# RWKV-7 inverse on one core: VectorE transposes 32-row blocks in place of half of TensorE's products

## The chip, the cores and the metric

One Trainium2 chip; the kernel is one program on one NeuronCore. The metric is the device time of one execution in microseconds. The times given are of single executions, with their median.

## The reference, cut to what matters

The program computes two transformer-like blocks on 272 tokens (256 and 16 learned ones), width 1024, in float32. The part that the change touches is the recurrence of the RWKV-7 time mix of the first block, with 16 heads of 64:

```python
def step(S, inp):
    r_t, w_t, k_t, v_t, a_t, b_t = inp
    sa = jnp.einsum("bhij,bhj->bhi", S, a_t)
    S = S * w_t[:, :, None, :] + sa[..., None] * b_t[:, :, None, :] + v_t[..., None] * k_t[:, :, None, :]
    y = jnp.einsum("bhij,bhj->bhi", S, r_t)
    return S, y
```

The kernel doesn't step through tokens. It takes them in chunks of 16, 128 and 128 and solves, for each head and chunk, one triangular system: with L the strictly lower triangular matrix of the products of a and b inside a chunk, it needs X = (I - L)^-1, applied to the part of `sa` that earlier chunks and the keys give.

## The kernel before

**Groups and chunks.** The 16 heads go in four groups g of four (q = 0 to 3). Each group has three chunks: c = 0 with 16 tokens, c = 1 and 2 with 128. `rk_score` makes the products, `rk_mask` (VectorE) masks them into `rk_lb` and `rk_lk`, and `rk_levels` builds the inverse by doubling the block: level n joins blocks of 2^n rows into blocks of 2^(n+1). For chunks of 128 both 64-row halves (TOP and BOTTOM) are inverted side by side in levels 0 to 5, and level 6 joins them. Chunk 0 has levels 0 to 3.

**What a level does.** Both the inverse so far and its transpose are kept: `rk_x` and `rk_xt`, tiles of 128 x (4 heads x 64) for chunks 1 and 2. Lines here are those of kernel.py.
- Level 0: VectorE writes `rk_xt` from the masked products (`rk_begin`, L2266, two products, a drain, an addition of the identity). TensorE transposes it by a product with the identity (`rk_under` at n = 0, L808), and ScalarE copies the result from PSUM to `rk_x` (L1706).
- Levels 1 to 4: TensorE makes `rk_lb` times `rk_x` (`rk_under`, L806); VectorE masks it from PSUM into `rk_ym` (L2292); TensorE makes two products of it (`rk_merge`), o (L826), what is added to `rk_x`, and ot (L828), what is added to `rk_xt`; VectorE adds both (L2308 and L2309). `rk_under` of the next level waits for `rk_x` alone, `rk_merge` of the next level for `rk_xt` too.
- Level 5 is alike, with o for the TOP half only, and the transpose goes to `rk_upper` and `rk_lower`. Level 6 is one product each way, with copies at L2290 and L2300.

Every float32 product stands in the trace as two LDWEIGHTS and two MATMUL instructions. Additions and masks on VectorE go through a helper and carry line L2001 (L2004 for three operands), copies and activations on ScalarE L1420.

**What sets the order.** Each engine runs its instructions in the order in which its own program issues them. `beside(host, guest)` weaves two generators: the host is `rk_levels(g)`, which yields once after each chunk's under and merge (slots), and the guest `rk_beside(g)` gives a slot number before each piece. TensorE and VectorE have a host and a guest each. For group g the guests carry the chain of group g-1 through its three chunks (`rk_right` L867, `rk_solve` L880 to L883, `rk_update` L896 to L898, `rk_output` L917 to L921, and for statistics `rk_mean` L930 and `rk_variance` L937), and they prepare group g+1 (`rk_turn` L764, `rk_score` L781, on VectorE `rk_mask` and `rk_begin`). In group 0 VectorE's guests are six pieces of `rk_prepare`, one of them due at each of slots 1 to 6. From group 2 on there is `rk_finish` of group g-2, with two reciprocals (L2341). `rk_output` waits for VectorE's `rk_state`, `rk_score(.., 1)` for VectorE's mask of `rk_score(.., 0)`. `fill` (L746) issues products that nothing reads: in group 0 four of them before each chunk of level 0, and some later.

**Around it.** The weights come by DMA through a ring of four slots; while the inverse runs no weight is consumed, and the ring is full. After group 3 the linear layers go on, each engine in its own order.

Of the kernel before, what the change touches and what calls it, by code (L numbers as in the profile page):

```python
# [12 lines left out]
ALU = mybir.AluOpType  # L13
# [203 lines left out]
def build(nc, stream, x_in, params, consts, decay, out):  # L217
    with ExitStack() as ctx:
# [209 lines left out]
        def rk_level_bank(c, i):  # L428


            C, B = CHUNKS[c][1], RK_SIDE[c]
            bank, at = ((4, 64 * i), (max(i - 1, 0), 0), (2 + max(i - 1, 0), 0))[c]
            return ps[0:C, bank, at:at + 4 * B].rearrange("p (q t) -> p q t", q=4)
# [24 lines left out]
        def masked(g, c, i):  # L458
            return MASKS.index((g, c, i)) + 1
# [105 lines left out]
        def _(pe):  # L565
# [219 lines left out]
            def rk_under(g, c, n):  # L785

                C = CHUNKS[c][1]
                if n == 0:
                    pe.wait_ge(S[f"rk_xt{c}_begun"], g + 1)
                    if g == 0:  # L790
                        pe.wait_ge(S["rk_masked"], masked(g, c, 1))
                    if c == 0 and g >= 2:
                        pe.wait_ge(S["rk_y_rooted"], g - 1)
                elif n == 1:
                    pe.wait_ge(S[f"rk_x{c}_begun"], g + 1)
                else:
                    pe.wait_ge(S[f"rk_x{c}_added"], g * RK_COUNT[c] + 2 * n - 2 - (c > 0))
                settle(C)
                o, lb, x = rk_level_bank(c, 0), rk_lb[g % 2][c], rk_x[c]
                for q in range(4):  # L800
                    if n == LEVELS - 1:
                        mm = pe.matmul(o[BOTTOM, q, :], lb[TOP, q, 0, BOTTOM], x[TOP, q, :], start=True, stop=True)
                    else:
                        for b in RK_BLOCKS[c]:
                            if n:
                                mm = pe.matmul(o[b, q, :], lb[b, q, 0, b], x[b, q, :], start=True, stop=True)  # L806
                            else:
                                mm = pe.matmul(o[b, q, :], rk_xt[g % 2][c][b, q, :], ident[b, b], start=True, stop=True)  # L808
                mm.then_inc(S[f"rk_under{c}_ready"], 1)

            def rk_merge(g, c, n):

                C, nl = CHUNKS[c][1], RK_LEVELS[c]
                if n > 1:
                    pe.wait_ge(S[f"rk_x{c}_added"], g * RK_COUNT[c] + 2 * n - 2)
                pe.wait_ge(S[f"rk_under{c}_masked"], g * (nl - 1) + n)
                settle(C)
                o, ot, xt, y = rk_level_bank(c, 1), rk_level_bank(c, 2), rk_xt[g % 2][c], rk_ym[c]
                for q in range(4):
                    if n == LEVELS - 1:  # L820
                        mm = pe.matmul(ot[TOP, q, :], y[BOTTOM, q, :], rk_lower[g % 2][c][BOTTOM, q, :],
                                       start=True, stop=True)
                        continue
                    for b in RK_BLOCKS[c] if n < nl - 1 else ():
                        if n < LEVELS - 2 or b == TOP:
                            pe.matmul(o[b, q, :], xt[b, q, :], y[b, q, :], start=True, stop=True)  # L826
                    for b in RK_BLOCKS[c]:
                        mm = pe.matmul(ot[b, q, :], y[b, q, :], xt[b, q, :], start=True, stop=True)  # L828
                mm.then_inc(S[f"rk_merge{c}_ready"], 1)

            def rk_levels(g):

                for n in range(LEVELS):
                    chunks = [c for c in RK_ORDER if n < RK_LEVELS[c]]
                    for c in chunks:
                        if g == n == 0:
                            fill(4, 4)
                        if n == LEVELS - 1:
                            pe.wait_ge(S["rk_masked"], masked(g + 1, 2, 1) if g < 3 else len(MASKS))
                            fill(7, 4)  # L840
                        rk_under(g, c, n)
                        yield
                    for c in chunks if n else ():
                        rk_merge(g, c, n)
                        yield
# [572 lines left out]
        def _(act):  # L1418
            def copy(o, i, scale=1.0):
                return act.activation(o, i, ACT.Copy, scale=scale)  # L1420
# [280 lines left out]
            for c in range(3):  # L1701
                rk_turned(0, c)
            for g in range(4):
                for c in RK_ORDER:
                    act.wait_ge(S[f"rk_under{c}_ready"], g * RK_LEVELS[c] + 1)
                    copy(rk_x[c][0:CHUNKS[c][1], :, :], rk_level_bank(c, 0)).then_inc(S[f"rk_x{c}_begun"], 1)  # L1706
                for c in range(3):
                    if c and g < 3:
                        rk_turned(g + 1, c - 1)
                    if g:  # L1710
                        rk_solved(g - 1, c)
                        rk_out(g - 1, c)
                if g < 3:
                    rk_turned(g + 1, 2)
                else:
                    copy(rk_lora[:, :, :], rk_gate_first)
                if g:
                    rk_spread(g - 1)
# [280 lines left out]
        def _(dve):  # L1999
            def tt(o, a, b, op):  # L2000
                return dve.tensor_tensor(o, a, b, op)  # L2001
# [264 lines left out]
            def rk_begin(g, c):  # L2266


                C, B, xt = CHUNKS[c][1], RK_SIDE[c], rk_xt[g % 2][c]
                dve.drain()  # L2270
                for b in RK_BLOCKS[c]:
                    tt(xt[b, :, :], rk_lb[g % 2][c][b, :, 0, b], tokens_of(const("level_0t")[b, 0:B], 4), ALU.mult)
                if c and g < 2:
                    dve.memset(rk_upper[g][c][BOTTOM, :, :], 0.0)
                dve.drain()
                tt(xt[0:C, :, :], xt[0:C, :, :], tokens_of(const("eye")[0:C, 0:B], 4), ALU.add
                   ).then_inc(S[f"rk_xt{c}_begun"], 1)

            def rk_levels(g):

                xt, upper, lower = rk_xt[g % 2], rk_upper[g % 2], rk_lower[g % 2]
                for c in RK_ORDER:
                    yield
                for n in range(1, LEVELS):
                    chunks = [c for c in RK_ORDER if n < RK_LEVELS[c]]
                    for c in chunks:
                        C, B = CHUNKS[c][1], RK_SIDE[c]
                        dve.wait_ge(S[f"rk_under{c}_ready"], g * RK_LEVELS[c] + (n + 1))
                        if n == LEVELS - 1:
                            ins = dve.tensor_copy(rk_ym[c][BOTTOM, :, :], rk_level_bank(c, 0)[BOTTOM, :, :])  # L2290
                        else:
                            ins = tt(rk_ym[c][0:C, :, :], rk_level_bank(c, 0), tokens_of(level[0:C, n, 0:B], 4), ALU.mult)  # L2292
                        ins.then_inc(S[f"rk_under{c}_masked"], 1)
                        yield
                    for c in chunks:
                        C = CHUNKS[c][1]
                        dve.wait_ge(S[f"rk_merge{c}_ready"], g * (RK_LEVELS[c] - 1) + n)
                        o, ot = rk_level_bank(c, 1), rk_level_bank(c, 2)
                        if n == LEVELS - 1:
                            ins = dve.tensor_copy(lower[c][TOP, :, :], ot[TOP, :, :])  # L2300
                        elif n == LEVELS - 2:
                            tt(rk_x[c][TOP, :, :], o[TOP, :, :], rk_x[c][TOP, :, :], ALU.add
                               ).then_inc(S[f"rk_x{c}_added"], 1)
                            tt(upper[c][TOP, :, :], ot[TOP, :, :], xt[c][TOP, :, :], ALU.add)
                            ins = tt(lower[c][BOTTOM, :, :], ot[BOTTOM, :, :], xt[c][BOTTOM, :, :], ALU.add)
                        else:
                            if n < RK_LEVELS[c] - 1:
                                tt(rk_x[c][0:C, :, :], o, rk_x[c][0:C, :, :], ALU.add).then_inc(S[f"rk_x{c}_added"], 1)  # L2308
                            ins = tt(xt[c][0:C, :, :], ot, xt[c][0:C, :, :], ALU.add)  # L2309
                        ins.then_inc(S[f"rk_x{c}_added"], 1)  # L2310
                        yield

# [100 lines left out]
            for c in range(3):  # L2413
                rk_mask(0, c, 1)
                if c:
                    rk_begin(0, c)
            rk_begin(0, 0)
            for g in range(4):
                beside(rk_levels(g), rk_beside(g))
# [396 lines left out]
```

## Time and profile before

| | us |
|---|---|
| times of three executions | 2116.26, 2116.26, 2118.11 |
| median | 2116.26 |
| the profiled execution, its own time | 2117.51 |
| its span in the trace | 2115.7 |
| granted TensorE clock, mean share of full speed | 0.979 |
| the inverse, from the first L808 to the last L821, on the span's clock | 353 to 530 |

The profile has an engine's busy time, the chain that ended last, groups of instructions, and a timeline. In a timeline row the number in brackets is how long the engine sat idle before the row and what it then waited for; a row merges neighbours of the same line, "x16" counting them. The end of a TensorE instruction is modelled, so the distance between starts is what it costs in a stream. "In group 2" means from 441.0 to 488.6 us.

### The profile page before, as it was taken

How to read it: one execution, taken by the hardware profiler on the slowest of the kernel's cores; microseconds unless marked ns; L12 is line 12 of the kernel's file. 1: busy time of each engine (PE TensorE's matmuls, PEld its weight loads, DVE VectorE, ACT ScalarE, POOL GpSimd, SP SyncE). 2: the span in 40 equal slices, each digit the busy share in tenths (PEclk: the TensorE clock that was granted, in tenths of full speed). 3: DMA queues.
4: the chain of work that ended last, by engine and by line, in shares of the span. 5: the costliest groups of instructions: out<-in, count | busy, mean ns of one | idle time of the engine just before them, and what ended most of it. 6: DMA issues, size and time to landing. Idle time of an engine off the chain costs nothing.

```text
span 2115.7 us, 43855 instructions
## 1 busy us (share of the span) xinstructions
PE 2011.4 (95%) x17474; PEld 1893.6 (90%) x17474; DVE 1056.3 (50%) x1608; ACT 924.2 (44%) x1613; POOL 1278.4 (60%) x528
## 2 busy tenths in 40 slices
PE   7999998999999999999989999999999989999997
PEld 7999687788899999998966999999998868898997
DVE  5770677566678617842474686030453243325431
ACT  4334552111343444344436444344446545656552
POOL 6887361000388877885720788776755544677885
PEclk9999999999999999999979999999999988999999
DMA  7444331000244544543310454543453332344552
GB/s 279 166 174 178 119 120 61 2 3 3 100 160 178 179 160 159 178 179 140 142 58 9 163 188 179 199 160 142 158 219 132 113 116 96 124 179 147 191 183 76
DMA packets 40935, 291.44 MB, mean 138 GB/s; under 512 B 4448, under 2 KB 5728, under 8 KB 5856
## 3 DMA queue, kind: packets, MB, share of 16 engines
q1 hardware_dynamic: 40656, 288.40, 37.7%
q8 instruction: 108, 1.77, 0.3%
q10 hardware_dynamic: 144, 1.05, 0.1%
q14 instruction: 27, 0.22, 0.0%
HBM read 288.38 MB, written 1.05 MB: 137 GB/s over the span
## 4 chain that ended last, share of the span: by engine, by line
PE 32%; issue 28%; POOLq 19%; POOL 18%; ACT 1%; DVE 1%; DMA 0%; DVEq 0%; SPq 0%; ACTq 0%
POOLq L1979 18%; POOL w_low L1975 18%; PE ps L617 10%; PE ps L625 9%; PE ps L621 9%; PE ps L1355 2%; PE ps L1343 1%; PE ps L1333 1%; PE ps L729 0%; POOLq L1974 0%; DMA X<-x_in 0%; ACT units L1881 0%; ACT units L1420 0%; POOLq L1991 0%; DVE units L2001 0%
## 5 line engine op out<-in xcount | busy, mean ns | idle before, releaser
L1975 POOL TENSOR_TENSOR w_low<-wring,w_high 128x1024 fp32r<-128x1024 f32 x524 | 1278.2, 2454 | 816.1 <-ACT w_high L1420 786.1
L617 PE MATMUL ps<-in_high,w_high 128*128 128x256 f32 (+1 forms) x2856 | 831.2, 291 | 33.8 <-DVE in_low L2001 12.9
L625 PE MATMUL ps<-in_high,w_low 128*128 128x256 f32 (+1 forms) x2856 | 820.7, 287 | 0.0
L621 PE MATMUL ps<-in_low,w_high 128*128 128x256 f32 (+1 forms) x2856 | 819.1, 287 | 0.0
L1420 ACT ACTIVATE w_high<-wring 128x1024 fp32r<-128x1024 f32 x524 | 542.2, 1055 | 278.1 <-PE ps L617 273.2
L617 PEld LDWEIGHTS ps<-in_high,w_high 128*128 128x128 f32 x2856 | 546.1, 191 | 46.6 <-issue 36.7
L625 PEld LDWEIGHTS ps<-in_high,w_low 128*128 128x128 f32 x2856 | 546.2, 191 | 0.0
L621 PEld LDWEIGHTS ps<-in_low,w_high 128*128 128x128 f32 x2856 | 545.8, 191 | 0.5
L617 PE MATMUL ps<-hid_high,w_high 128*128 128x272 f32 (+1 forms) x880 | 254.6, 289 | 0.0
L625 PE MATMUL ps<-hid_high,w_low 128*128 128x272 f32 (+1 forms) x880 | 250.4, 284 | 0.0
L621 PE MATMUL ps<-hid_low,w_high 128*128 128x272 f32 (+1 forms) x880 | 250.2, 284 | 0.0
L2001 DVE TENSOR_TENSOR hid_low<-hidden,hid_high 128x272 f32 (+1 forms) x88 | 215.7, 2451 | 13.0 <-issue 2.4
L2004 DVE SCALAR_TENSOR_TENSOR X<-ps,X 128x272 f32<-128x272 f32 (+1 forms) x64 | 27.7, 433 | 333.1 <-PE ps L625 333.1
L1561 ACT ACTIVATE silu_out<-ps 128x272 f32<-128x272 f32 (+1 forms) x88 | 34.7, 394 | 301.9 <-DVE ps L2001 301.9
L621 PEld LDWEIGHTS ps<-hid_low,w_high 128*128 128x128 f32 x880 | 165.7, 188 | 0.7
L617 PEld LDWEIGHTS ps<-hid_high,w_high 128*128 128x128 f32 x880 | 165.4, 188 | 0.7
L625 PEld LDWEIGHTS ps<-hid_high,w_low 128*128 128x128 f32 x880 | 165.5, 188 | 0.0
L2039 DVE CAST hid_high<-hidden 128x272 f32 (+1 forms) x88 | 97.0, 1103 | 17.2 <-issue 17.2
L2001 DVE TENSOR_TENSOR ps<-ps,rms 128x272 f32<-128x272 f32 (+1 forms) x176 | 73.9, 436 | 61.2 <-PE ps L625 60.0
L1420 ACT ACTIVATE AL<-ps 128x272 f32<-128x272 f32 (+5 forms) x95 | 39.7, 434 | 138.8 <-PE ps L625 46.6
L2004 DVE SCALAR_TENSOR_TENSOR conv_out<-ps,par,conv_out 128x255 f32<-128x255 f32 x88 | 42.5, 482 | 46.5 <-ACT conv_out L1550 37.7
L1508 ACT ACTIVATE units<-ps 128x256 f32<-128x256 f32 x69 | 26.4, 383 | 85.1 <-PE ps L625 85.0
(339 smaller groups left out, 2566.9 us busy)
## 6 DMA issues: line engine op xcount, KB each, us to landing
wring<-stream SPq DMA_DIRECT2D x270, 1024.0 KB, 4.8
con<-consts SPq DMA_DIRECT2D x1, 2199.0 KB, 16.0
X<-x_in SPq DMA_DIRECT2D x1, 1088.0 KB, 7.6
units<-decay ACTq DMA_DIRECT2D x1, 1024.0 KB, 4.8
out<-AL SPq DMA_DIRECT2D x1, 1024.0 KB, 4.7
AL<-stream SPq DMA_DIRECT2D x2, 256.0 KB, 19.7
par<-params SPq DMA_DIRECT2D x1, 187.0 KB, 4.9
con<-consts SPq DMA_DIRECT2D x1, 130.0 KB, 7.5
```

The lines of the kernel that those rows point to most:

```text
L617: mm = pe.matmul(o, wh, high(k), start=(k == 0), stop=False)
L621: mm = pe.matmul(o, wh, low(k), start=False, stop=False)
L625: mm = pe.matmul(o, wl, high(k), start=False, stop=(k == kt - 1))
L1355: mm = pe.matmul(ps[:, 7, :], v, pt.rearrange("p q t -> p (q t)"), start=(i == 0), stop=(i == len(of_keys) - 1))
L1420: return act.activation(o, i, ACT.Copy, scale=scale)
L1508: act.activation(put(i), ps[:, BANK[tile], 0:size], func(i)).then_inc(S["act_emptied"], 1)
L1561: act.activation(silu_out[:, p % 2, tokens], ps[:, (base + 2 * p) % 4, 0:size], ACT.Silu).then_inc(S["act_emptied"], 1)
L1975: pool.tensor_tensor(w_low[:, (half + h) % SPLIT_RING, :], wring[:, slot, h * HALF * P:(h + 1) * HALF * P], w_high[:, (half + h) % SPLIT_R ...
L1979: pool.drain()
L2001: return dve.tensor_tensor(o, a, b, op)
L2004: return dve.scalar_tensor_tensor(out=o, in0=a, scalar=scalar, in1=b, op0=op0, op1=op1)
L2039: dve.tensor_copy(hid_high[:, tile, tokens], hidden[:, p:p + 1, tokens])
```

## The change

Where the blocks have up to 32 rows, `rk_xt` of chunks 1 and 2 is got from `rk_x` (or at level 0 `rk_x` from `rk_xt`) by a transpose on VectorE, which turns each 32 x 32 block where it stands. At level 0 the 16 products with the identity and both ScalarE copies go, and `rk_first` (VectorE) writes `rk_x`: for group 0 before `rk_begin(0, 0)`, for later groups at level 6 of the group before, behind the copies of L2290. At levels 1 to 4 the products ot of chunks 1 and 2 go, and VectorE's addition to `rk_xt` is replaced by a drain and a transpose. Level 5, level 6 and chunk 0 keep what they do; chunk 0's block is written as rows 0 to 16 throughout. Semaphore counts follow.

```diff
@@ rk_under, TensorE
+                if n == (c > 0) and g == 0:
+                    pe.wait_ge(S["rk_masked"], masked(g, c, 1))
                 if n == 0:
-                    pe.wait_ge(S[f"rk_xt{c}_begun"], g + 1)
-                    if g == 0:
-                        pe.wait_ge(S["rk_masked"], masked(g, c, 1))
-                    if c == 0 and g >= 2:
+                    pe.wait_ge(S["rk_xt0_begun"], g + 1)
+                    if g >= 2:
                         pe.wait_ge(S["rk_y_rooted"], g - 1)
@@ rk_merge, TensorE
-                    for b in RK_BLOCKS[c] if n < nl - 1 else ():
-                        if n < LEVELS - 2 or b == TOP:
-                            pe.matmul(o[b, q, :], xt[b, q, :], y[b, q, :], start=True, stop=True)
+                    if n == LEVELS - 2:
+                        pe.matmul(o[TOP, q, :], xt[TOP, q, :], y[TOP, q, :], start=True, stop=True)
+                    elif c == 0 and n < nl - 1:
+                        pe.matmul(o[:, q, :], xt[0:C, q, :], y[0:C, q, :], start=True, stop=True)
                     for b in RK_BLOCKS[c]:
-                        mm = pe.matmul(ot[b, q, :], y[b, q, :], xt[b, q, :], start=True, stop=True)
+                        if c and n < LEVELS - 2:
+                            mm = pe.matmul(o[b, q, :], xt[b, q, :], y[b, q, :], start=True, stop=True)
+                        else:
+                            mm = pe.matmul(ot[b, q, :], y[b, q, :], xt[b, q, :], start=True, stop=True)
@@ rk_levels, TensorE
-                        rk_under(g, c, n)
+                        if n or c == 0:
+                            rk_under(g, c, n)
@@ the groups, ScalarE
-                for c in RK_ORDER:
-                    act.wait_ge(S[f"rk_under{c}_ready"], g * RK_LEVELS[c] + 1)
-                    copy(rk_x[c][0:CHUNKS[c][1], :, :], rk_level_bank(c, 0)).then_inc(S[f"rk_x{c}_begun"], 1)
+                act.wait_ge(S["rk_under0_ready"], g * RK_LEVELS[0] + 1)
+                copy(rk_x[0][0:CHUNKS[0][1], :, :], rk_level_bank(0, 0)).then_inc(S["rk_x0_begun"], 1)
@@ new, VectorE
+            def rk_first(g, c):
+                dve.transpose(rk_x[c], rk_xt[g % 2][c]).then_inc(S[f"rk_x{c}_begun"], 1)
@@ rk_levels, VectorE: behind the masks of a level
+                    if n == LEVELS - 1 and g < 3:
+                        dve.drain()
+                        for c in chunks:
+                            rk_first(g + 1, c)
@@ rk_levels, VectorE: behind the merge, levels 1 to 4
-                            ins = tt(xt[c][0:C, :, :], ot, xt[c][0:C, :, :], ALU.add)
+                            if c:
+                                dve.drain()
+                                ins = dve.transpose(xt[c], rk_x[c])
+                            else:
+                                ins = tt(xt[c][0:C, :, :], ot, xt[c][0:C, :, :], ALU.add)
@@ before group 0, VectorE
+            dve.drain()
+            for c in (1, 2):
+                rk_first(0, c)
             rk_begin(0, 0)
```

## Rows read from the trace of the kernel before

**Rows 1.** Busy time by engine, page of the profile, whole span.

```profile
PE 2011.4 (95%) x17474; PEld 1893.6 (90%) x17474; DVE 1056.3 (50%) x1608; ACT 924.2 (44%) x1613; POOL 1278.4 (60%) x528
```

**Rows 2.** Stretches: length, busy us (instructions) per engine, clock, DMA share, GB/s.

```profile
352.00:394.00 42.00, 34.73 (x702) 29.84 (x703) 32.57 (x78) 3.57 (x9) 0.00 (x0) 1.00 0.01 2
394.00:441.00 47.00, 44.94 (x864) 37.92 (x863) 25.90 (x65) 7.80 (x18) 0.00 (x0) 1.00 0.01 2
441.00:488.60 47.60, 45.54 (x874) 38.52 (x873) 30.86 (x71) 7.23 (x18) 0.00 (x0) 1.00 0.01 3
488.60:530.00 41.40, 38.94 (x813) 33.71 (x812) 24.74 (x61) 5.04 (x13) 0.00 (x0) 1.00 0.01 3
```

**Rows 3.** Groups by form, 352 to 530: count, busy us, mean ns, idle before.

```profile
L828 PE MATMUL ps<-group,in_parts 64*64 64x64 f32 x320 | 19.7, 220 | 0.0
```

**Rows 4.** Line 808: count, ns min/median/max, first and last start, forms.

```profile
L808 PE MATMUL ps<-con,group x80: 171/218/267, 352.8 to 443.3; 64*64 64x64 f32 x64, 16*16 16x16 f32 x16
```

**Rows 5.** TensorE timeline, group 2: start, us, what, idle before and releaser.

```profile
445.86 0.33 PE L826 MATMUL ps<-in_parts,group 64*64 64x64 f32 x4
...
446.94 0.29 PE L917 MATMUL ps<-in_parts 16*64 16x16 f32 x4
...
457.21 0.44 PE L917 MATMUL ps<-AL,in_parts 128*64 128x128 f32 x4 [0.48 <-DVE small L2001]
...
468.35 1.13 PE L781 MATMUL ps<-AL 64*128 64x256 f32 x8 [1.06 <-DVE AL L2001]
...
478.63 1.13 PE L781 MATMUL ps<-AL 64*128 64x256 f32 x8 [0.43 <-DVE AL L2001]
```

**Rows 6.** VectorE timeline, group 2, same columns.

```profile
447.05 0.76 DVE L2001 TENSOR_TENSOR group<-ps,group 128x256 f32<-128x256 f32 x2 [0.55 <-PE ps L828]
...
456.14 0.41 DVE L2001 TENSOR_TENSOR small<-ps,small 128x256 f32<-128x256 f32 x1
456.63 0.42 DVE L2001 TENSOR_TENSOR small<-small 128x256 f32<-128x256 f32 x1
...
467.08 1.22 DVE L2001 TENSOR_TENSOR AL<-ps,con 128x1024 f32<-128x1024 f32 x1
```

**Rows 7.** VectorE, bounds of one instruction: a short one and the longest.

```profile
351.98 0.27 DVE L2274 MEMSET group<- 64x256 f32 x1
...
L2341 DVE RECIPROCAL in_parts<-in_parts 128x272 f32<-128x272 f32 x5 | 9.2, 1849 | 0.1
```

**Rows 8.** VectorE, then TensorE, timelines at the start of group 0.

```profile
356.30 1.36 DVE L2001 TENSOR_TENSOR AL<-AL 128x544 f32<-128x544 f32 x2
...
367.61 0.76 DVE L2001 TENSOR_TENSOR group<-ps,group 128x256 f32<-128x256 f32 x2 [0.68 <-PE ps L828]
...
350.84 1.16 PE L746 MATMUL ps<-con 128*128 128x128 f32 x8
...
356.28 1.16 PE L746 MATMUL ps<-con 128*128 128x128 f32 x8
357.36 0.36 PE L808 MATMUL ps<-con,group 16*16 16x16 f32 x8
...
360.12 0.33 PE L826 MATMUL ps<-in_parts,group 64*64 64x64 f32 x4 [1.02 <-DVE in_parts L2001]
```

**Rows 9.** VectorE timeline where groups meet: 0 with 1, 2 with 3.

```profile
392.67 0.98 DVE L2290 COPY in_parts<-ps 64x256 f32<-64x256 f32 x2
393.92 0.97 DVE L2300 COPY group<-ps 64x256 f32<-64x256 f32 x2 [0.27 <-PE ps L821]
...
488.63 0.42 DVE L2300 COPY group<-ps 64x256 f32<-64x256 f32 x1 [1.29 <-PE ps L821]
```

**Rows 10.** Stretches before the inverse and where the clock fell, as rows 2.

```profile
346.00:350.00 4.00, 1.57 (x18) 1.00 (x20) 2.73 (x4) 0.00 (x0) 0.00 (x0) 1.00 0.00 0
...
993.00:995.00 2.00, 0.34 (x2) 0.00 (x0) 0.60 (x1) 1.35 (x2) 0.00 (x0) 1.00 0.30 127
995.00:997.00 2.00, 0.00 (x0) 0.00 (x0) 1.92 (x3) 0.13 (x1) 0.00 (x0) 0.72 0.00 0
```

More of the change, by code:

```diff
@@ L2275, in rk_begin @@
                 dve.drain()
-                tt(xt[0:C, :, :], xt[0:C, :, :], tokens_of(const("eye")[0:C, 0:B], 4), ALU.add
-                   ).then_inc(S[f"rk_xt{c}_begun"], 1)
+                ins = tt(xt[0:C, :, :], xt[0:C, :, :], tokens_of(const("eye")[0:C, 0:B], 4), ALU.add)
+                if c == 0:
+                    ins.then_inc(S["rk_xt0_begun"], 1)
+            def rk_first(g, c):
+                dve.transpose(rk_x[c], rk_xt[g % 2][c]).then_inc(S[f"rk_x{c}_begun"], 1)
             def rk_levels(g):
@@ L2287, in rk_levels @@
                         C, B = CHUNKS[c][1], RK_SIDE[c]
-                        dve.wait_ge(S[f"rk_under{c}_ready"], g * RK_LEVELS[c] + (n + 1))
+                        dve.wait_ge(S[f"rk_under{c}_ready"], g * RK_LEVELS[0] + n + 1 if c == 0 else g * (LEVELS - 1) + n)
                         if n == LEVELS - 1:
```

## The prediction

> **What bounds the kernel now.** The page first: TensorE is busy for 95% of the span, VectorE for half [rows 1]. That is an average over many stages, so I cut the inverse into its four groups [rows 2]. There is next to no DMA there, the granted clock is 1.00 throughout, and TensorE is busy 44.94 of 47.00 us in group 1, 45.54 of 47.60 in group 2 and 38.94 of 41.40 in group 3. VectorE has 24.7 to 30.9 us of work in these. Group 0 is another case: TensorE 34.73 of 42.00, VectorE 32.57. So three groups are bound by TensorE's stream of small products, and the first partly by VectorE. As TensorE's instructions run in program order, a product taken out lets everything behind it move up, until something behind it waits for VectorE. Those waits decide how much comes back; I read them in the timelines [rows 5, 6].
>
> **What goes.** The groups by form show 320 instructions of 64*64 at L828 for one buffer, and a second row with 320 for the other, the products ot of levels 1 to 5 [rows 3]: two chunks, four groups, 16 each per level, for five levels. Four of five levels go: 512. L808 has 64 of 64*64 in the even groups [rows 4] and as many in the odd ones: 128 more. In a stream such an instruction costs not its 220 ns but its distance to the next: merge of chunk 1 at level 1, 32 instructions (both products), begins at 445.86 and the next piece at 446.94 [rows 5]; less about 0.15 for its start and end, that is 0.93 us, 29 ns each. So 640 x 29 ns = 18.8 us of TensorE's stream go, 4.7 per group, 0.94 at each of levels 0 to 4. ScalarE's eight copies at level 0 go too; they are off the path, TensorE having other work meanwhile, and I give them nothing.
>
> **What comes.** VectorE gets 40 transposes of 128x256: 32 in place of additions, 8 new, each pair behind a drain. No row of before has a transpose. The bounds are a memset of 0.27 us and a reciprocal of 1.85 us [rows 7]. I take 0.42 us, the time of a plain 128x256 operation in the row at 456.63 [rows 6], since data go through once in both; both ends stay for the range. The Trainium skill (VectorE: DVE Perf Modes, "The three transpose paths") gives 311 ns for 128x128 in bf16; no run here shows that, and for twice the elements it would be an estimate between 0.31 and 0.62.
>
> A drain: two independent additions take 0.76 us together, so the second begins 0.34 behind the first; the pair with a drain between (456.14 and 456.63) is 0.49 apart [rows 6]. A drain costs 0.15, and the pair of an addition and a transpose 0.91 where the two additions took 0.76. The Trainium skill says otherwise (VectorE: DVE Perf Modes, "The DRAIN you can't avoid"): the pipe is emptied behind every operation anyway and chaining doesn't avoid it. By that rule the drains would be free, and the 32 of levels 1 to 4 would take 4.8 us less of VectorE than I reckon; with half of them on the path the gain would be 2.4 us larger. The rows contradict it here, and I go by them.
>
> **How much comes back: group 2, step by step.** I shift each piece by what is gone ahead of it and hold it where its releaser is late. *Level 0*: 0.94 gone, but `rk_solve` now stands close behind `rk_right` and waits for VectorE's copy between them; 0.6 come back. *Level 1*: another 0.94, but `rk_output` of chunk 0 waits 0.4 for the state, which stands behind VectorE's masks. The under of level 2 comes 1.5 earlier. *Level 2*: `rk_output` of chunk 1 (457.21) already waits 0.48 for `rk_state`, which stands behind chunk 1's additions [rows 5, 6]. These begin when chunk 1's merge ends, now 0.47 sooner, and take 0.15 more: it starts 1.8 earlier in all, TensorE waiting 1.4. *Level 3*: `rk_score` at 468.35 waits 1.06 for the mask that VectorE begins at 467.08, again behind chunk 1's additions [rows 5, 6]. It starts 2.15 earlier and waits 1.85. *Level 4*: VectorE had idled between chunk 1's and chunk 2's additions, so both halves of the merges count; `rk_score` at 478.63 starts 3.0 earlier. So 3.0 of 4.7 come back: 0.6 at level 0 and 2.4 behind it. The rule is that what is behind chunk 2's merge waits for VectorE work started by chunk 1's.
>
> *Group 1* has the same waits: 2.4 behind its level 0. *Group 3* has no preparation of a next group to fill TensorE, so after about 0.6 per level its chain under, mask, merge, addition becomes the bound: 0.6 + 2.2. *Ends of groups*: between L2290 and L2300 VectorE idles 1.29 us at the end of group 2, so drain and two transposes (0.9) are hidden. At the end of group 0 the idle is 0.27 [rows 9], and they cost 0.6.
>
> *Group 0* begins with a loss. VectorE's chain is the bound: `rk_prepare` at 356.30 runs on to the mask for which TensorE's merge at 360.12 waited 1.02 us [rows 8]. A drain, two transposes and `rk_begin` behind them put it 0.95 later. VectorE's next idle is before 367.61 [rows 8]; from there levels 2 to 4 bring 2.3, and the end takes 0.6 of 0.94 at level 0 of group 1. Net: -0.95 + 2.3 - 0.4 = +0.95.
>
> **Sum**: 0.95 + 2.4 + 3.0 + 2.8 = 9.15 us. Nothing behind the inverse hides it, as the weights lie ready and each engine goes on in order. The profiled execution took 2117.51 (span 2115.7), which gives 2108.4; it stands 1.25 above the median of 2116.26, so the median becomes **2107.1**.
>
> **Rivals.**
> *A. All comes back* (18.8 us, 2097.5). For it: TensorE's 95%. Against: TensorE already waits in three places per group for VectorE, and I only shorten the cover. Chance 0.07.
> *B. The transpose costs twice and more, and the gain is lost.* About five of ten transposes per group are on the path, 20 in all. At 0.72 us the gain falls by 6 to 3.1, at 0.88 it is nil. So from 0.66 to 1.1 us the time is within 4.2 us of before: 2112 to 2120. For it: nothing here shows the operation. Chance 0.14.
> *C. Slower through VectorE.* Place: the additions of levels 1 to 4; price: that of the reciprocal, 1.85 us. Then 20 x 1.43 = 28.6 more, less 9.15: 19.5 slower, 2135.7. It decides from 0.88 on and shows as slower from 1.1. Chance 0.06.
> *D. Slower through the clock.* The three `fill`s at level 0 (1.08 us each, 356.28 to 357.36) now run one after another from 350.84 [rows 8] to 354.1, since no product stands between them, and TensorE then idles until about 357.2, when `rk_begin(0, 0)` ends: 3.1 us, and again for some 2 us before the first merge, which moves from 360.12 to 361.1. In the trace the clock fell from 1.00 to 0.72 and on to its lower level (1.2 GHz) after TensorE had been busy 0.34 of 2 us and 0.00 of the next 2; it did not fall where it was busy 1.57 of 4 us [rows 10]. The Trainium skill (TensorE: Matmul & The Clock Gate, "Part 1: The HAM clock gate") has the same rule, that an idle TensorE is put back to half rate. So a fall is about as likely as not. Its price: at 1.2 GHz a stream of 29 ns products takes 58 ns, but until 367 VectorE is the bound and hides that, so I give it 0 to 2 us. It decides if the clock stays low for over 9 us of busy TensorE past 367; through all of group 0 it would cost up to 25 us, 16 more than is gained: 2132. Against: the products are dense there. Chance 0.06.
>
> **Numbers.** The forecast (gain 4.3 to 14) has 0.67, A 0.07, B 0.14, C 0.06, D 0.06. About 0.2% (4.2 us) is what a measurement of this kernel can tell from no change. Faster by more than that: 0.67 + 0.07 = 0.74; within: 0.14; slower: 0.12. The range leaves out the full return, C and D: from 2100 (16 back) to 2115.5, where the transpose costs 0.84.
>
> **What would show it.** L828 of 64*64 down from 640 to 128, none at L808. TRANSPOSE rows of about 0.42 us, 40 of them: 0.8 would mean B, over 1.1 C. The stretch from 353 to 530 shorter by 9, its group 2 by 3.0; TensorE's waits for VectorE up from about 2 to about 4 us in groups 1 and 2, at `rk_output` of chunk 1 1.4 and at `rk_score` 1.85. Group 0's first mask about 0.95 later, and the granted clock around 354 to 361 either 1.00 or at 1.2 GHz with no loss behind 367. Wrong would be: a stretch unchanged though transposes are short, or one shorter by 15 and more, or the difference outside this stretch.

## The result: slower, by the clock

The changed kernel took 2130.12 us in the median of four executions (2127.39 to 2133.25), before 2116.38; the ratio is 1.0063, with a 95% interval of 1.0046 to 1.0081. Ten more executions of it later gave 2127.29 (2119.05 to 2139.0) beside 2116.74, ratio 1.0059 (1.0035 to 1.0082). A ratio is the time of the kernel at hand over that of before on the same chip; all those below are within one per cent of 1, and what counts is whether their interval leaves 1 out. I had forecast 2107.1, faster.

The page of the changed kernel, parts 1 and 2, shows what moved:

```profile
PE 2012.9 (95%) x16834; PEld 1891.3 (89%) x16834; DVE 1060.3 (50%) x1616; ACT 921.8 (43%) x1605; POOL 1280.2 (60%) x528
...
PEclk9999998899899999999989999999999988999999
```

The 640 TensorE instructions are gone (17474 in [rows 1], 16834 here), and its busy time still grew, from 2011.4 to 2012.9 us. That is what a lower clock would do, and the stretches below show where it was low. The clock line has 8s in the seventh, eighth and eleventh slices, where the inverse runs and ends; in the profile of before the whole inverse had 1.00 [rows 2]. Stretches of the changed kernel, cut where the granted clock changes (length, busy us and count of PE, PEld, DVE, ACT, POOL, then clock, DMA share, GB/s):

```profile
346.90:350.30 3.40, 1.68 (x20) 0.86 (x16) 1.79 (x2) 0.00 (x0) 0.00 (x0) 1.00 0.00 0
...
350.30:357.10 6.80, 6.09 (x27) 5.27 (x28) 6.36 (x13) 0.00 (x0) 0.00 (x0) 0.50 0.00 0
...
394.70:398.10 3.40, 2.76 (x44) 2.49 (x44) 2.86 (x8) 0.21 (x1) 0.00 (x0) 1.00 0.00 0
398.10:411.80 13.70, 13.70 (x178) 11.92 (x176) 4.23 (x12) 1.42 (x4) 0.00 (x0) 0.50 0.01 2
...
425.40:428.80 3.40, 1.71 (x22) 1.30 (x24) 2.58 (x6) 0.00 (x0) 0.00 (x0) 1.00 0.00 0
428.80:432.20 3.40, 3.40 (x38) 2.42 (x34) 1.10 (x1) 0.38 (x1) 0.00 (x0) 0.50 0.00 0
447.40:492.20 44.80, 40.80 (x707) 33.80 (x706) 32.26 (x74) 6.29 (x15) 0.00 (x0) 1.00 0.01 2
...
493.70:497.10 3.40, 3.00 (x78) 2.65 (x77) 2.88 (x5) 0.59 (x2) 0.00 (x0) 1.00 0.02 5
497.10:507.30 10.20, 10.20 (x142) 9.38 (x144) 5.60 (x13) 0.58 (x2) 0.00 (x0) 0.50 0.01 2
534.60:548.30 13.70, 13.70 (x83) 10.31 (x84) 5.61 (x7) 2.33 (x5) 2.35 (x1) 0.50 0.00 0
```

At 0.50 the clock is at its lower level, 1.2 GHz. There TensorE is busy without a gap (13.70 of 13.70 us): it is the bound, at half speed. The falls come at starts of groups 1 and 3, in the middle of group 1, twice in group 0 and behind group 3. The first, at 350.30, lies ahead of every instruction that the change touches. The kernel before ran the same products there, 1.23 us earlier on its span's clock and as busy as the first row above, and kept its clock:

```profile
345.67:349.07 3.40, 1.68 (x20) 0.86 (x16) 1.80 (x2) 0.00 (x0) 0.00 (x0) 1.00 0.00 0
```

So one and the same stretch can be followed by a fall in one execution and not in another, and chance has a part here. The repeat of the changed kernel (e8 below) says so too: its profile has falls at the starts of groups 1 and 2 and none in group 3. What TensorE did before a fall is in the rows ahead of the 0.50 ones. It was half idle before two of them (1.68 and 1.71 busy us of 3.40). Before the falls at the starts of groups 1 and 3 it wasn't: 2.76 and 3.00 of 3.40, in small products with short waits.

Group 2 is the piece that had 1.00 throughout, and it did what was forecast. From one level 6 to the next (line L821), first before, then changed:

```profile
440.61 0.97 PE L821 MATMUL ps<-in_parts 64*64 64x64 f32 x13
...
487.92 0.97 PE L821 MATMUL ps<-group,in_parts 64*64 64x64 f32 x13
...
526.41 1.14 PE L821 MATMUL ps<-in_parts 64*64 64x64 f32 x16
```

```profile
447.41 1.14 PE L821 MATMUL ps<-in_parts 64*64 64x64 f32 x16
...
492.20 1.14 PE L821 MATMUL ps<-group,in_parts 64*64 64x64 f32 x16
```

47.31 us became 44.79, 2.5 less. In a second profile of the changed kernel (the repeat, e8) group 3 had the full clock, and 38.49 became 36.08, 2.4 less:

```profile
499.46 1.14 PE L821 MATMUL ps<-group,in_parts 64*64 64x64 f32 x16
...
535.54 1.14 PE L821 MATMUL ps<-in_parts 64*64 64x64 f32 x16
```

The waits are the forecast ones too: TensorE's idle time in group 2 is 4.00 us (44.80 less 40.80, the stretch from 447.40) where it was 2.06 [rows 2]. TensorE's timeline in group 2 of the changed kernel, to be held against [rows 5]:

```profile
462.52 0.44 PE L923 MATMUL ps<-AL,in_parts 128*64 128x128 f32 x4 [1.06 <-DVE small L2006]
...
473.38 1.13 PE L781 MATMUL ps<-AL 64*128 64x256 f32 x8 [1.71 <-DVE AL L2006]
...
482.91 1.14 PE L781 MATMUL ps<-AL 64*128 64x256 f32 x8 [0.62 <-DVE AL L2006]
```

**Time against the clock.** Every execution has its mean granted clock, and 2 x (1 - clock) x span is the time at the lower level, called low time from here on. The 97 executions of before that ran beside all these kernels have 72 to 110 us of it, mean 88, and their times, 2111.0 to 2123.8, rise by 0.45 us per us of it (a straight line fitted). The 14 of the changed kernel have 119 to 171 us, mean 142, slope 0.41. On these lines, at 85 us for both, before takes 2116.0 and the changed kernel 2104.8: 11.2 less. That is an extrapolation for the changed kernel, whose least is 119; by the scatter of its 14 points it is good to about 3 us. So two sizes stand against each other: 54 us more at the low level, at 0.45 each some 24 us, against 11 to 13 us less of work. The means of all executions are 2117.4 and 2128.2, 10.8 apart.

### The profile page after: what moved, and what is told of

Its sections match the earlier page's. It is cut to its first block, busy times and chain, and to the rows that moved or that the text cites. A ratio compares the mean times of both kernels' runs of the same rounds, so it can differ in the third digit from the quotient of the medians.

```text
span 2125.6 us, 42611 instructions
## 1 busy us (share of the span) xinstructions
PE 2012.9 (95%) x16834; PEld 1891.3 (89%) x16834; DVE 1060.3 (50%) x1616; ACT 921.8 (43%) x1605; POOL 1280.2 (60%) x528
## 4 chain that ended last, share of the span: by engine, by line
PE 31%; issue 28%; POOLq 19%; POOL 18%; ACT 1%; DVE 1%; DMA 0%; DVEq 0%; SPq 0%; ACTq 0%
POOLq L1984 18%; POOL w_low L1980 18%; PE ps L617 9%; PE ps L625 9%; PE ps L621 9%; PE ps L1361 1%; PE ps L1349 1%; PE ps L1339 1%; PE ps L729 0%; POOLq L1979 0%; DMA X<-x_in 0%; ACT units L1886 0%; ACT units L1426 0%; POOLq L1996 0%; DVE units L2006 0%
## 6 DMA issues: line engine op xcount, KB each, us to landing
AL<-stream SPq DMA_DIRECT2D x2, 256.0 KB, 18.6
```

## The experiments

Theory 1: the work is less, as forecast, and the loss is the granted clock. Theory 2, the rival: VectorE's drains, transposes and later start cost it, whatever the clock. Each kernel has one profile, of one of its executions, and it isn't always a typical one; where that matters it is said.

**e1, TensorE's products kept.** VectorE as changed; TensorE issues what the change had taken out, and nobody reads it.

```diff
                         if n or c == 0:
                             rk_under(g, c, n)
+                        else:
+                            pe.wait_ge(S[f"rk_x{c}_begun"], g + 1)
+                            for q in range(4):
+                                for b in RK_BLOCKS[c]:
+                                    pe.matmul(rk_level_bank(c, 0)[b, q, :], rk_xt[g % 2][c][b, q, :], ident[b, b],
+                                              start=True, stop=True)
...
                         if c and n < LEVELS - 2:
+                            pe.matmul(ot[b, q, :], y[b, q, :], xt[b, q, :], start=True, stop=True)
```

> The changed kernel, with TensorE still issuing the 640 instructions that the change took out (their results are read by nobody) and VectorE as changed. Theory 1 (the granted clock): TensorE is as dense as before, so the clock stays at 1.00 through the inverse and the time is 2114 to 2120 us, a little over before for the drains. Theory 2 (VectorE's drains, transposes and the later start cost it, whatever the clock): 2127 us or more, since all of VectorE's additions are in and nothing of TensorE's is gone.

Measured: 2116.73 us, ratio 0.9997 (0.9977 to 1.0017). Its groups 1 to 3:

```profile
397.70:446.10 48.40, 45.83 (x866) 38.82 (x866) 28.39 (x70) 6.86 (x15) 0.00 (x0) 1.00 0.01 2
446.10:494.20 48.10, 45.57 (x867) 38.57 (x866) 32.42 (x74) 6.29 (x15) 0.00 (x0) 1.00 0.01 3
494.20:533.10 38.90, 37.05 (x794) 32.45 (x793) 23.85 (x58) 4.24 (x10) 0.00 (x0) 1.00 0.01 3
```

All that the change adds to VectorE is in, and it costs 1.0, 0.8 and 0.4 us where 47.37, 47.31 and 38.49 were before. Theory 2 falls for the whole. With TensorE as dense as before the clock stood in groups 1 to 3, and the low time over the ten executions, 86 us on average, is no more than before's 89 on that chip. I had expected it to stand through the whole inverse, and that it didn't: the profile, of the slowest of the ten (2122.77), has a fall of 6.8 us from 355.0 on, in group 0, and one of 10.2 us behind group 3.

**e2, levels 1 to 4 alone; e3, level 0 alone.** e2 has the hunk of `rk_merge` and the drain and transpose behind it, with level 0 as before; e3 has `rk_first` and no products at level 0, with levels 1 to 4 as before. e3 against the changed kernel:

```diff
-                    elif c == 0 and n < nl - 1:
-                        pe.matmul(o[:, q, :], xt[0:C, q, :], y[0:C, q, :], start=True, stop=True)
-
+                    elif n < nl - 1:
+                        for b in RK_BLOCKS[c]:
+                            pe.matmul(o[b, q, :], xt[b, q, :], y[b, q, :], start=True, stop=True)
...
-                        if c and n < LEVELS - 2:
-                            mm = pe.matmul(o[b, q, :], xt[b, q, :], y[b, q, :], start=True, stop=True)
-                        else:
-                            mm = pe.matmul(ot[b, q, :], y[b, q, :], xt[b, q, :], start=True, stop=True)
+                        mm = pe.matmul(ot[b, q, :], y[b, q, :], xt[b, q, :], start=True, stop=True)
...
-                            if c:
-                                dve.drain()
-                                ins = dve.transpose(xt[c], rk_x[c])
-                            else:
-                                ins = tt(xt[c][0:C, :, :], ot, xt[c][0:C, :, :], ALU.add)
+                            ins = tt(xt[c][0:C, :, :], ot, xt[c][0:C, :, :], ALU.add)
```

Expected of e2:

> Only levels 1 to 4 changed; level 0 as before (product with the identity, ScalarE's copies). Theory 1a (the clock falls because the dense products of level 0 are gone at the start of each group): no fall in groups 1 to 3, 2107 to 2111 us. Theory 1b (it falls because the stream is thinner everywhere): at least two falls between 353 and 530 us remain and the time is 2116 to 2130 us. Theory 2 (VectorE): 2122 to 2128.

Expected of e3:

> Only level 0 changed; levels 1 to 4 as before. Theory 1a: the clock falls at the starts of groups as in the changed kernel, 2118 us or more. Theory 1b: few or no falls, the gain of level 0 alone (3 x 0.6 less 0.95 at the start), 2114 to 2117 us. Theory 2: 2116 to 2119.

Measured: e2 2115.02, ratio 0.9993 (0.9971 to 1.0015); e3 2131.47, ratio 1.0074 (1.0047 to 1.0102). The small part of the change does the harm, 128 instructions of 640: e3 lies in the range of theory 1a. e2 lies in none of its three ranges. Stretches of e3 around each fall:

```profile
396.10:399.50 3.40, 2.91 (x44) 2.49 (x42) 3.13 (x9) 0.21 (x1) 0.00 (x0) 1.00 0.00 0
399.50:416.60 17.10, 16.94 (x234) 14.99 (x234) 4.05 (x14) 1.80 (x5) 0.00 (x0) 0.50 0.01 2
450.70:454.10 3.40, 3.00 (x45) 2.38 (x43) 2.71 (x6) 0.93 (x2) 0.00 (x0) 1.00 0.00 0
454.20:474.70 20.50, 20.50 (x308) 18.27 (x310) 8.55 (x20) 1.78 (x5) 0.00 (x0) 0.50 0.01 2
505.40:508.80 3.40, 3.00 (x44) 2.41 (x42) 2.70 (x7) 0.93 (x2) 0.00 (x0) 0.99 0.00 0
508.80:519.00 10.20, 10.20 (x149) 9.55 (x146) 4.04 (x9) 0.57 (x2) 0.00 (x0) 0.50 0.01 3
```

Each of groups 1 to 3 begins with a fall. At these starts only the short chunk's pieces (16 rows), some waits and the fills are left once L808 is gone. e2 keeps L808 but wasn't free of falls: in its profile, of the slowest of ten executions (2124.92), the clock averaged 0.96, 0.93 and 0.91 over its three groups. Two of these falls, at 449.9 and 497.7, came after TensorE had been busy almost throughout:

```profile
446.50:449.90 3.40, 3.28 (x82) 2.91 (x79) 2.39 (x8) 0.20 (x1) 0.00 (x0) 1.00 0.02 5
494.30:497.70 3.40, 3.29 (x88) 2.91 (x84) 2.39 (x8) 0.20 (x1) 0.00 (x0) 1.00 0.02 5
```

So neither the busy time nor the count of instructions just before a fall tells that it comes; what in the stream does is open. e2 had 104 us at the low level on average, 15 more than before; with before's 88 it would stand, at 0.45 per us, at about 2109 (from its mean, 2116.2). So neither 1a (starts alone) nor 1b holds by itself: the starts are the worst place, the thinner stream of levels 1 to 4 a second one.

**e13, level 0 alone with its products kept.** e3 plus the first hunk of e1.

> Only level 0 changed, as in the kernel that took 2131 us, but TensorE still issues the products of level 0 with nobody reading them. Theory 1 (the loss of that kernel is the clock that falls when these products are missing): no falls in groups 1 to 3, 2114 to 2120 us. Theory 3 (its loss is VectorE's transposes and drains at the start of group 0 and at level 6): 2126 us or more, as without them.

Measured: 2122.13, ratio 1.0022 (1.0007 to 1.0037), 9 us less than e3 and 2 us above the range of theory 1, whose other half, no falls in groups 1 to 3, holds. Groups 1 to 3:

```profile
398.10:445.70 47.60, 45.55 (x867) 38.51 (x867) 27.60 (x70) 6.85 (x15) 0.00 (x0) 1.00 0.01 2
445.70:493.00 47.30, 45.25 (x868) 38.22 (x867) 31.60 (x74) 6.28 (x15) 0.00 (x0) 1.00 0.01 3
493.00:531.40 38.40, 36.72 (x793) 32.18 (x792) 23.13 (x58) 4.23 (x10) 0.00 (x0) 1.00 0.01 3
```

They are as long as before's, so the transposes at level 6 are hidden, and at the starts of these groups it is the missing products that let the clock fall. Of the 4 us that remain against before, its profile has 2.5 in group 0: from VectorE's 128x1088 operation that ends `rk_inputs` to the first L821 it takes 55.6 us, before 53.1. It has 6.8 us of low clock there, between 352 and 362, and its first mask, which waits for level 0's products behind the transposes, comes 2.46 us later. Its low time is 97 us on average, 8 more than before. Which of the two brought the other wasn't tried by itself.

**e4, fills of 128x128 in the waits; e5 to e7, wide float32 fills.** A fill is a product that nobody reads. e4 adds single 128x128 ones to the changed kernel; e5 (changed kernel), e6 (before) and e7 (e2) add wide ones. From e5:

```diff
+            def wide(n, bank):
+                for _ in range(n):
+                    pe.matmul(ps[0:32, bank, 0:512], ident[:, 0:32], con[:, 0:512], start=True, stop=True)
...
+                        wide((1, 3, 0)[c], 1)
                         rk_output(before, c)
```

Expected of e4:

> The changed kernel with idle-time products of 128x128 that nobody reads, set where TensorE waits for VectorE: 1 before each merge of chunk 1 at levels 1 to 4, 1 at each chunk of level 0 from group 1 on, 1 before the solve and the output of chunk 0, 4 before the output of chunk 1, 5 before the second scores of chunk 1. Theory 1: the clock is held at 1.00 in groups 1 to 3 and a part of the 9 us comes out: 2108 to 2114 us. Theory 2: the fills only add work, 2128 to 2135 us.

Expected of e5:

> The changed kernel with other idle-time products, which nobody reads: all 128 rows of the array, 512 columns in one go (about 0.45 us each). One at level 0 and one before the solve and one before the output of chunk 0 in groups 1 to 3, three before the output of chunk 1, four before the second scores of chunk 1, three and two before the first merges of group 0, two before each of the second scores ahead of group 0, one before each solve behind group 3. Theory 1 (the fall of the clock is the whole loss): the clock is held at 1.00 in groups 1 to 3, the four groups take 52, 46, 46 and 38 us between their last levels, and the time is 2106 to 2112 us. Theory 2 (something else slows the changed kernel): the clock is held, yet it is 2118 us or more.

Expected of e6:

> The kernel before with the same idle-time products ahead of group 0, at the first merge of chunk 1 in group 0, at level 0 of groups 1 to 3, before the solves of chunk 0 and behind group 3 (not at the outputs and scores, where it has hardly a wait). Theory 1: its clock was at 1.00 through the inverse already, so it only gets the work of the fills: 2116 to 2122 us. If it gets faster, the clock in before was no less at risk than in the changed kernel.

Expected of e7:

> Levels 1 to 4 changed and level 0 as before, with the idle-time products of the first of these kernels. Theory 1: the clock is held; level 0's products cost 0.6 us a group more than without them, but its VectorE work is less: 2106 to 2112 us, within 3 us of the first kernel. Theory 2: 2118 us or more.

Measured: e4 2125.84, ratio 1.0034 (1.0006 to 1.0062), anywhere from 2117.1 to 2139.8; its three groups had a clock of 0.87, 0.84 and 0.78. Too few, then: it lies above theory 1's range, and with the clock not held it says nothing on theory 2. e5 2135.52, 1.0085 (1.0063 to 1.0106); e6 2127.9, 1.0049 (1.0030 to 1.0068); e7 2134.32, 1.0073 (1.0056 to 1.0091). All three lie above the ranges of theory 1. The clock of e5 was held in groups 1 to 3, as the first stretch below shows for group 1, but groups 1 and 2 are 50.4 us and not 46 (44.8 was the changed kernel's group 2 at the full clock), since a fill costs about 0.92 us (three in 2.76) and not the 0.45 that I had put:

```profile
399.70:450.10 50.40, 49.70 (x727) 35.52 (x727) 28.30 (x70) 6.86 (x15) 0.00 (x0) 1.00 0.01 2
...
466.33 2.76 PE L751 MATMUL ps<-con 128*32 128x512 f32 x6
```

Ten per group are 9 us, more than the waits hold. These three therefore say that the clock can be held, and nothing of theory 1's total. By the clause of e5 for theory 2 (held, yet over 2118) it was met; the row of the fill says why that is no evidence for it.

**e8, the changed kernel again.**

> The changed kernel itself again, beside the others on this chip. Theory 1: its falls depend on where the clock's decisions come in its groups, so its runs spread over several us, all above 2120 us; a run's time rises by about half of the time that the clock was low. Theory 2: a fixed time of 2127 to 2131 us whatever the clock.

Measured: 2127.29, 2119.05 to 2139.0. Two of ten lie below 2120, a little outside the expectation; the time follows the low time, from 119 to 171 us of it, with a slope of 0.42. Theory 2's fixed time falls. Its profile is of its fastest execution (2119.05).

**e9 to e12, bfloat16 fills.** Same places, operands read as bfloat16: one instruction of 512 columns where float32 takes two.

```diff
-                    pe.matmul(ps[0:32, bank, 0:512], ident[:, 0:32], con[:, 0:512], start=True, stop=True)
+                    pe.matmul(ps[0:32, bank, 0:512], ident[:, 0:16].bitcast(mybir.dt.bfloat16),
+                              con[:, 0:256].bitcast(mybir.dt.bfloat16), start=True, stop=True)
```

Expected of e9:

> The changed kernel with idle-time products in the same places as the kernel with the wide float32 ones, but in bfloat16 (one instruction of 512 columns, by what float32r products of 272 columns take, 0.13 us, an estimate of 0.25 us each instead of about 0.95), and eight more where TensorE waits ahead of group 0. Theory 1 (the clock is the whole loss): granted clock 1.00 in groups 1 to 3, their times 46 to 47, 46 to 47 and 37 us, total 2108 to 2115 us. Theory 2: the clock held and still 2120 us or more.

Expected of e10:

> The kernel before with the same bfloat16 products where a bank is free for them (two before each of the second scores ahead of group 0, three at the first merge of group 0, one at level 0 and before the solve of chunk 0 in groups 1 to 3, one before each solve behind group 3). Theory 1: the clock was not at fault there, 2115 to 2120 us, with a smaller spread than the 2111 to 2123 us of before.

Expected of e11:

> Levels 1 to 4 changed, level 0 as before, with bfloat16 idle-time products in the waits of the outputs and scores, before the solves and at the start of group 0. Theory 1: clock held, 2108 to 2114 us.

Expected of e12:

> The changed kernel with two bfloat16 products at level 0 of groups 1 to 3, one before the solve and the output of chunk 0, and one only before the output of chunk 1 and the second scores of chunk 1. Theory 1 with the falls decided at the starts of groups: as good as with three and four there, 2108 to 2115 us. If the later waits matter as well: falls in the middle of groups, 2115 to 2125 us.

Measured: e9 2124.54, 1.0026 (1.0009 to 1.0042), its groups at 0.84, 0.90 and 0.84, a miss; e10 2120.16, 1.0006 (0.9988 to 1.0025), at the upper end of its range, but its times spread from 2113.6 to 2129.0, wider than before's and not narrower as expected; e11 **2112.57, 0.9963 (0.9949 to 0.9977)**, faster by 0.4% and in its range; e12 2119.12, 1.0014 (0.9991 to 1.0037), in the range of its second case and with falls at the starts of all three groups and in the middle of two (in the profile, of an execution of 2129.29). Without L808 no set of fills that I tried was both cheap and sufficient. With L808 kept, the cheap ones held the clock in groups 1 to 3 in all three profiles (e11, e14, e15). e10 is the control for them: with before's stream its few fills gain nothing. And e11 has 87 us of low time on average, before 89, so what it gains is work taken out and not clock.

**e14 and e15, the best version again.** e11 with four more fills behind group 3 (e14) and unchanged (e15).

```diff
+            quick(4, 7)
             pe.wait_ge(S["rk_masked"], len(MASKS))
             pe.wait_ge(S["rk_y_squared"], 3)
```

Expected of e14:

> Levels 1 to 4 changed, level 0 as before, bfloat16 idle-time products, and four more of them directly behind group 3, where TensorE waits for VectorE's last copies and the clock fell for 13.7 us from 524 us on. Theory 1: without that fall 3 to 6 us less than the kernel without these four: 2106 to 2111 us. Rival: the fall comes a little later all the same, 2112 to 2114.

Expected of e15:

> The same kernel without these four again, for its interval: 2111 to 2118 us, ratio to before 0.995 to 0.998.

Measured: 2112.07, 0.9975 (0.9957 to 0.9992), and 2112.05, 0.9974 (0.9955 to 0.9993). The gain repeats. The four fills bring nothing that shows, as e14's rival had it by its number, but not for its reason: no fall came a little later in e14's profile (last row below), and e15's, without the four, has none behind group 3 either. e11's fall there comes and goes by itself. Groups 1 to 3 of e14 and what follows:

```profile
392.50:438.30 45.80, 43.98 (x748) 35.25 (x748) 27.05 (x66) 7.52 (x17) 0.00 (x0) 1.00 0.01 3
438.30:484.10 45.80, 44.05 (x749) 35.29 (x748) 31.81 (x71) 6.95 (x17) 0.00 (x0) 1.00 0.01 2
484.10:521.10 37.00, 34.81 (x671) 29.03 (x670) 23.70 (x57) 4.90 (x12) 0.00 (x0) 1.00 0.01 3
521.10:545.00 23.90, 22.73 (x226) 16.11 (x226) 16.11 (x27) 7.39 (x16) 5.02 (x2) 1.00 0.01 1
```

Against 47.37, 47.31 and 38.49 that is 1.6, 1.5 and 1.5 us less per group, fills included, and the clock at 1.00. That is 4.6 of the 6 us by which e14 and e15 are faster.

## Why the prediction was wrong

**What failed** is the term for the granted clock. The sum has none: it takes every instruction at its price at the full clock. Rival D put the clock at a chance of 0.06. It looked for a fall in one place, TensorE's idle time ahead of group 0, priced it at 0 to 2 us, and dismissed the rest with "the products are dense there". In its place the runs show 142 us of low time on average against before's 88, at 0.45 each some 24 us, more than the 11 to 13 us of work that went; and e3 and e13 show that it is the 128 instructions of level 0, missing at the starts of groups, that cost 13 us by themselves. D's 2132, for a clock low through all of group 0, lies near the measured 2130 by luck: in group 0 the profile has 6.8 us of low clock, besides the 6.8 ahead of 357, and the rest lies in groups 1 and 3 and behind them. The rows that I took as examples of a fall [rows 10] have an almost idle TensorE; I had none for a busy one. The runs show falls out of stretches with 2.76 to 3.29 busy us of 3.40, and stretches of 10 to 20 us at 1.2 GHz with TensorE busy throughout. The Trainium skill (TensorE: Matmul & The Clock Gate, "Part 1: The HAM clock gate") puts the low state down to a TensorE that has been idle or little busy, and in one case to many short idles between groups of products. The falls at 398.1 and 497.1 fit the latter; those of e2, out of 3.28 and 3.29 busy us of 3.40, go beyond it, since busy time alone didn't hold the clock there. Nor did I use the sign in the code: the fills of before stand where its stream is thin, and level 0's products stood at the start of each group for free.

**What was right, at the full clock.** The terms, in the order of the prediction:
- Removed: 128 of 64*64 left at L833, none at L808, 640 instructions fewer, as reckoned. (640 x 29 ns is 18.6 us and not 18.8, a slip that changes nothing.)
- The transpose: taken as 0.42 us; 0.445 and 0.424 measured. That agrees with the Trainium skill (VectorE: DVE Perf Modes, "The three transpose paths"), whose figure gave an estimate of 0.31 to 0.62. Groups by form of the changed kernel:

```profile
L2326 DVE STREAM_TRANSPOSE group<-group 128x256 f32<-128x256 f32 x16 | 7.1, 445 | 1.5
...
L2288 DVE STREAM_TRANSPOSE group<-group 128x256 f32<-128x256 f32 x4 | 1.5, 424 | 0.2
```

- The drain: taken as 0.15. The VectorE timeline below has 0.50 from an addition to the transpose behind the drain, where two additions were 0.34 apart. So the drains aren't free. That they would be is what the prediction read out of the Trainium skill (VectorE: DVE Perf Modes, "The DRAIN you can't avoid"), which has the pipe emptied behind every operation. The same section says that an operation that isn't held starts earlier, and with that the 0.34, less than the 0.42 of one operation, agrees.

```profile
366.06 0.40 DVE L2006 TENSOR_TENSOR group<-ps,group 128x256 f32<-128x256 f32 x1
366.56 0.45 DVE L2326 STREAM_TRANSPOSE group<-group 128x256 f32<-128x256 f32 x1
366.93 0.39 DVE L2006 TENSOR_TENSOR group<-ps,group 128x256 f32<-128x256 f32 x1
```

- Group 2: 3.0 forecast, 2.5 measured; group 3: 2.8 and 2.4. The waits at `rk_output` of chunk 1, 1.4 and 1.06; at `rk_score`, 1.85 and 1.71. The step-by-step shifting holds to 0.5 us a group. Group 1 never ran at the full clock in a profile of the changed kernel.
- Group 0's first mask: 0.95 later forecast, 0.84 measured (19.54 and 20.38 us behind VectorE's 128x1088 operation that ends `rk_inputs`). What group 0 gives as a whole isn't known, as no profile of the changed kernel had it at the full clock. The nearest are e9 and e12, the changed kernel with cheap fills, which had: 52.3 us from that operation to the first L821 where before has 53.1, 0.8 less with the fills in it, against -0.95 + 2.3 = 1.35 forecast. The -0.4 that the prediction adds doesn't follow from its own words either, since 0.94 less 0.6 leaves +0.3.
- The sum, 9.15: at equal low time the two lines give 11.2. That is good to about 3 us, and I don't count it as better than the groups', which were at 1.00.

Rivals A and C are out: group 2 gave back 2.5 of 4.7, and the transpose costs what a plain operation does. B's time didn't come either.

## What to carry to other kernels

A stream of small products can be the bound and at the same time what keeps TensorE's clock up: before taking products out, look at what is left where the stream is thinnest (here the starts of the groups), and price the change at the lower clock too, about 0.45 us per us spent there. Split such a change by where its products stand: the four fifths of it at levels 1 to 4, with cheap fills in the waits, gave 0.25 to 0.37%; without fills they gave nothing that could be measured (e2); the fifth at level 0 alone cost 13 us. A result of under one per cent wants each execution's granted clock beside its time.

## What the runs showed that I had not expected

- The clock fell with TensorE busy for 2.76 of 3.40 us (changed kernel) and for 3.28 (e2), and stayed at 1.2 GHz for up to 20.5 us with TensorE busy throughout (e3).
- The kernel before isn't free of this: its executions spread from 2111.0 to 2123.8 us, with 72 to 110 us at the lower level.
- A float32 fill of 128 rows x 512 columns costs 0.92 us, so that ten of them cost more than the clock that they hold.
